# Forty-eight low-part subtractions on GpSimd, and GpSimd's loads on ScalarE's queue

## The reference

```python
def first_block(x, ...):
    for l in range(DEPTH):                       # DEPTH = 2
        h = rms_norm(x, norm_g[l])
        (gu, gv, gz, rq, rk, rv, rz, dq, dk, dv, dz,
         a_f, b_f, a_b, b_b) = jnp.split(h @ w_in[l], IN_OFFSETS, axis=-1)   # eleven blocks of 512 columns
        y_a = gmlp_branch(...)                   # token mixing with a 128x128 matrix
        y_b = retention_branch(...)              # rotary, decay masks, both directions
        y_c = gdn_branch(...)                    # delta rule: inverse of a 64x64 triangle, scan over 4 chunks
        proj = jnp.einsum("bsnw,nwd->bsnd", branches, w_branch_out[l])
        gates = jax.nn.sigmoid(jnp.einsum("bsd,dne->bsne", h, w_gate[l]))
        x = x + jnp.sum(gates * proj, axis=2) @ w_out[l]
    return rms_norm(x, final_norm_g)
```

## Time and profile before

| what | value |
|---|---|
| median of three runs | 1969.39 us |
| span of the profiled execution, its first to its last instruction (the page gives no other time of that execution) | 1968.4 us |
| TensorE (PE) busy | 1799.5 us, 91% |
| VectorE (DVE) busy | 1154.7 us, 59% |
| ScalarE (ACT) busy | 875.8 us, 44% |
| GpSimd (POOL) busy | 11.4 us, 1% |
| the 16 DMA engines | 148 GB/s on average |
| mean granted TensorE clock | 0.947 |

### The profile page before, as it was taken

The page is one execution under the profiler, slowest core; times in us unless marked ns, Lnnn a source line. Parts: engine busy times, 40 slices in busy tenths (PEclk is TensorE's granted clock), DMA queues, the critical chain, the costliest instruction groups (busy, mean ns, idle before and its releaser), DMA issues.

```text
span 1968.4 us, 24530 instructions
## 1 busy us (share of the span) xinstructions
PE 1799.5 (91%) x10424; PEld 1486.3 (76%) x10424; DVE 1154.7 (59%) x1578; ACT 875.8 (44%) x1017; POOL 11.4 (1%) x24
## 2 busy tenths in 40 slices
PE   7899899898999988999898989899989998769996
PEld 5777788687877876888686757788868886558885
DVE  4776885556778656545556534554555455774554
ACT  5443444346244434444445633444444444644442
POOL 0000000000000000000000000000000000000000
PEclk9899999888999998999899968899999998879998
DMA  6231445432123644555442212555545554234552
GB/s 253 84 108 66 145 154 192 160 129 86 67 102 129 226 152 150 187 187 192 161 171 99 94 43 94 184 186 192 192 164 191 190 193 160 94 131 171 174 189 86
DMA packets 41438, 291.75 MB, mean 148 GB/s; under 512 B 4609, under 2 KB 4737, under 8 KB 7153
## 3 DMA queue, kind: packets, MB, share of 16 engines
q1 hardware_dynamic: 38720, 280.16, 39.9%
q0 software_dynamic: 2608, 10.03, 1.4%
HBM read 289.12 MB, written 1.05 MB: 147 GB/s over the span
## 4 chain that ended last, share of the span: by engine, by line
PE 75%; DVE 16%; ACT 5%; issue 3%; POOL 0%; DVEq 0%; ACTq 0%
PE pg L436 22%; PE pg L437 21%; PE pg L438 21%; DVE wl L1383 4%; PE ps L634 3%; PE ps L516 2%; ACT wh L993 2%; DVE x L1841 1%; PE ps L889 1%; PE ps L887 1%; DVE arena L1504 1%; DVE arena L1507 1%; PE ps L674 0%; DVE arena L1999 0%; DVE sm L1460 0%
## 5 line engine op out<-in xcount | busy, mean ns | idle before, releaser
L1383 DVE TENSOR_TENSOR wl<-raw,wh 128x2048 fp32r<-128x2048 f32 x266 | 608.6, 2292 | 518.6 <-ACT wh L993 517.6
L436 PE MATMUL pg<-wh,hTh 128*128 128x512 f32 (+1 forms) x2160 | 852.4, 395 | 43.6 <-DVE hTl L1424 11.3
L437 PE MATMUL pg<-wl,hTh 128*128 128x512 f32 (+1 forms) x2160 | 836.9, 387 | 0.0
L438 PE MATMUL pg<-wh,hTl 128*128 128x512 f32 (+1 forms) x2160 | 835.9, 387 | 0.0
L993 ACT ACTIVATE wh<-raw 128x2048 fp32r<-128x2048 f32 x266 | 508.9, 1914 | 525.6 <-PE pg L438 516.7
L436 PEld LDWEIGHTS pg<-wh,hTh 128*128 128x128 f32 x2160 | 412.8, 191 | 138.6 <-issue 46.3
L438 PEld LDWEIGHTS pg<-wh,hTl 128*128 128x128 f32 x2160 | 411.6, 191 | 83.1
L437 PEld LDWEIGHTS pg<-wl,hTh 128*128 128x128 f32 x2160 | 412.3, 191 | 76.7
L1072 ACT ACTIVATE arena<-pg,sm 128x512 f32<-128x512 f32 (+1 forms) x49 | 33.0, 673 | 163.4 <-PE pg L438 163.4
L516 PE MATMUL ps<-cst,x 128*128 128x128 f32 x128 | 27.6, 402 | 50.7 <-DVE x L1841 34.1
L516 PEld LDWEIGHTS ps<-cst,x 128*128 128x128 f32 x128 | 24.6, 215 | 53.6 <-DVE x L1841 36.2
(11 more groups left out here) (320 smaller groups left out, 1168.9 us busy)
## 6 DMA issues: line engine op xcount, KB each, us to landing
raw<-weights SPq DMA_DIRECT2D x266, 1024.0 KB, 4.8
arena<-wide POOLq DMA_DIRECT2D x9, 512.0 KB, 3.5
x<-x_in SPq DMA_DIRECT2D x1, 1024.0 KB, 5.0
cst<-const_tables POOLq DMA_DIRECT2D x1, 1024.0 KB, 5.1
plainh<-dist_tables POOLq DMA_DIRECT2D x2, 512.0 KB, 4.8
arena<-gate_mix POOLq DMA_DIRECT2D x1, 1024.0 KB, 5.8
y_out<-x POOLq DMA_DIRECT2D x1, 1024.0 KB, 4.5
arena<-token_mix POOLq DMA_DIRECT2D x2, 256.0 KB, 3.8
```

Of the source, the lines that this page charges most:

```text
L436: pe.matmul(dst, lh, rh, start=first, stop=False)
L437: pe.matmul(dst, lh, rl, start=False, stop=False)
L438: return pe.matmul(dst, ll, rh, start=False, stop=last)
L1383: tt(wl[:, slot, :], raw[:, u % RAW_SLOTS, :], wh[:, slot, :], ALU.subtract)\
```

## The change

The 48 filler units' low parts are written by GpSimd instead of VectorE. The semaphore `split_low` becomes two, `low_dve` and `low_pool`, and TensorE and SyncE wait for the one that belongs to the unit. GpSimd's loads and its store move into ScalarE's program, at places where ScalarE's own order or an added wait makes them safe.

```diff
+LAYER_UNITS, FF_UNITS, HYB_UNITS, REC_UNITS = 44, 34, 30, 12
+POOL_UNITS = frozenset([LAYER_UNITS * l + u for l in range(DEPTH) for u in range(6, 22)]
+                       + [LAYER_UNITS * DEPTH + FF_UNITS + u for u in range(10, 22)]
+                       + [LAYER_UNITS * DEPTH + 3 * FF_UNITS + HYB_UNITS + u for u in range(4, 8)])
+def low_of(u):
+    by_pool = len([v for v in POOL_UNITS if v <= u])
+    return ("low_pool", by_pool) if u in POOL_UNITS else ("low_dve", u + 1 - by_pool)
...
 (TensorE, in prepare and gemm)
-                        pe.wait_ge(sem["split_low"], st.used + 1)
+                        low, count = low_of(st.used)
+                        pe.wait_ge(sem[low], count)
...
 (ScalarE)
+                if l == DEPTH - 1:
+                    act.dma_start(V(13824), wide[6]).then_inc(sem["final_g_landed"], 16)
                 gemm(D, (512,), ("evac_act",), read_gates(1, 1))
+                act.wait_ge(sem["params_used"], l + 1)
+                act.dma_start(par[:, :], params[l + 1]).then_inc(sem["params_landed"], 16)
...
+            def ffn(name, post, last_of_block=False):
                 features_of_x(lambda k: name[:, k:k + 1], X_AT)
+                load_gain(post)
+                if last_of_block:
+                    act.dma_start(V(11776, 2048).rearrange("p (t n) -> p t n", t=2),
+                                  gate_mix.rearrange("t p n -> p t n")).then_inc(sem["mix_landed"], 16)
+                    act.wait_ge(sem["params_used"], DEPTH + 1)
+                    act.dma_start(par[:, :], params[3]).then_inc(sem["params_landed"], 16)
...
 (hybrid and recurrent, behind features_of_x: load_gain(1), load_gain(4))
+            def load_gain(i):
+                act.dma_start(V(13824), wide[i]).then_inc(sem["wide_landed"], 16)
...
                 features_of_x(lambda k: fp("norm_g")[:, k:k + 1])
+                act.dma_start(DIST, dist).then_inc(sem["dist_landed"], 16)
                 small_w(16, fp("small_w"))
                 gdn()
+                act.dma_start(LN_GAINS, wide[7 + l]).then_inc(sem["wide_landed"], 16)
+                act.dma_start(TOKEN_MIX, token_mix[l]).then_inc(sem["mix_landed"], 16)
                 retention()
...
+            c.wait("x_ready", 2)
+            act.dma_start(out.rearrange("a (m p) d -> p (a m) d", p=P), x[:, :, :]).then_inc(sem["out_landed"], 16)
+            act.wait_ge(sem["out_landed"], 16)
...
 (VectorE, in pump)
-                    dve.wait_ge(sem["split_high"], u + 1)
-                    tt(wl[:, slot, :], raw[:, u % RAW_SLOTS, :], wh[:, slot, :], ALU.subtract)\
-                        .then_inc(sem["split_low"], 1)
+                    if u not in POOL_UNITS:
+                        dve.wait_ge(sem["split_high"], u + 1)
+                        tt(wl[:, slot, :], raw[:, u % RAW_SLOTS, :], wh[:, slot, :], ALU.subtract)\
+                            .then_inc(sem["low_dve"], 1)
...
 (SyncE)
-                    sp.wait_ge(sem["split_low"], u - RAW_SLOTS + 1)
+                    low, count = low_of(u - RAW_SLOTS)
+                    sp.wait_ge(sem[low], count)
...
 (GpSimd, behind its first two loads; its later loads and the store are gone from here)
+            for u in sorted(POOL_UNITS):
+                slot = u % SPLIT_SLOTS
+                pool.wait_ge(sem["split_high"], u + 1)
+                pool.tensor_tensor(wl[:, slot, :], raw[:, u % RAW_SLOTS, :], wh[:, slot, :], ALU.subtract)\
+                    .then_inc(sem["low_pool"], 1)
```

More of the change, by code:

```diff
@@ L276, in program @@
             "rope_done", "row_done", "rs_ready", "rv_ready", "sc_masked", "sc_ready", "small_done",
-            "small_read", "small_w_high", "small_w_low", "split_high", "split_low", "sq_done", "sq_free",
+            "small_read", "small_w_high", "small_w_low", "split_high", "low_dve", "low_pool", "sq_done", "sq_free",
             "sq_ready", "ssd_decay", "ssd_done", "ssd_mask", "state_ready", "state_scaled", "sv_done",
@@ L1183, in retention, with merge_out @@
                 prepare(4)
-            def merge_out():
+            def merge_out(l):
                 def read_gates(n, first=0):
@@ L1226, in gemm_out @@
                 pump(st.used + 3)
-            def ffn(name):
+            def ffn(name, post, last_of_block=False):
                 features_of_x(lambda k: name[:, k:k + 1], X_AT)
+                load_gain(post)
[4 more added lines that the diff above has]
+                    act.dma_start(par[:, :], params[3]).then_inc(sem["params_landed"], 16)
                 hid = V(0, 2 * FF).rearrange("p (m f) -> p m f", m=M)
@@ L1241, in hybrid @@
                 features_of_x(lambda k: spar("g2")[:, k:k + 1])
+                load_gain(1)
                 z = V(10240, 2048).rearrange("p (m f) -> p m f", m=M)
@@ L1315, in recurrent @@
                 features_of_x(lambda k: rp("g2")[:, k:k + 1])
+                load_gain(4)
                 def read(i, pair, w):
@@ L1355, in _ @@
                 features_of_x(lambda k: fp("norm_g")[:, k:k + 1])
+                act.dma_start(DIST, dist).then_inc(sem["dist_landed"], 16)
                 small_w(16, fp("small_w"))
                 gdn()
+                act.dma_start(LN_GAINS, wide[7 + l]).then_inc(sem["wide_landed"], 16)
+                act.dma_start(TOKEN_MIX, token_mix[l]).then_inc(sem["mix_landed"], 16)
                 retention()
-                merge_out()
+                merge_out(l)
             act.wait_ge(sem["params_landed"], 16 * 2)
             small_w(24, spar("small_w"))
-            ffn(spar("g0"))
+            ffn(spar("g0"), 0)
             hybrid()
-            ffn(spar("g4"))
+            ffn(spar("g4"), 2, True)
             act.wait_ge(sem["params_landed"], 16 * 3)
-            ffn(rp("g0"))
+            ffn(rp("g0"), 3)
             recurrent()
-            ffn(rp("g4"))
+            ffn(rp("g4"), 5)
+            c.wait("x_ready", 2)
+            act.dma_start(out.rearrange("a (m p) d -> p (a m) d", p=P), x[:, :, :]).then_inc(sem["out_landed"], 16)
+            act.wait_ge(sem["out_landed"], 16)
         @block.vector
@@ L2085, in _ @@
         def _(pool):
-            c = Counter(pool, sem, None)
             pool.dma_start(ident, const[:, 0:P]).then_inc(sem["ident_landed"], 16)
```

## The result

The change made the kernel slower: 2027.78 us median (2024.35 to 2033.16, four runs) against 1970.43 us (1969.28 to 1972.56) for the kernel before on the same chip. The ratio is 1.0292, interval 1.0274 to 1.0309. The forecast was 1986 us, with a range up to 2002. So the direction was right, and the size was too small by a factor of 3.5: 58.8 us more in the profiled span (2027.2 against 1968.4), where 16.9 were counted.

What follows compares the result with a forecast made beforehand. TensorE, busy 91% of the span, was taken to bound the kernel, low parts costing only where it waits. Span 1968.4 + 13.6 for two layers + 3.3 for the hybrid mixer + 1.0 around it gave 1986 us, range 1951 to 2002.

Steps and rivals of the forecast that it cites:

- GpSimd's 4.6 us: Filler units: time GpSimd takes for one low part, its two inputs coming in one after the other, 4.6 us.
- The loads at nothing: ScalarE's queue: eighteen moved transfers, about 6 us of issue, are hidden and cost nothing.
- Units with little room: Filler units with 4.55 to 4.8 us between high part and first use; the tightest gives back 0.6 us a layer.
- masks and start of the inverse: Each layer: GpSimd holds L1566's second operation, 2.2 us, and operations among L1577 to L1580, 2.3 us.
- waits that go: Each layer: TensorE's waits at L634, L674 and L690, met by no GpSimd operation, end; -2.1 us.
- scan's end: Each layer: L1634 with two SBUF inputs starts late behind GpSimd, TensorE waiting at its end; 2.0 us.
- rotary step: Each layer: two GpSimd units fall into two-input operations; one hold costs 0.1 us, two 4.7, middle 2.4.
- hybrid mixer: Four units beside sixteen heads: one mask hold of 2.2 us, the others 1.5 as mean, less 2.7 gained; +3.3 us.
- I take the middle: Start of the inverse: between nothing and a 4.6 us hold, 2.3 us; the rotary step likewise 2.4.
- far end: Each layer: the hold's upper values, 9.2 us in the inverse and 4.7 in the rotary step, making 16.0 us.
- recorded rival: Whole kernel: holds at 16.0 us a layer plus the hybrid's 3.3, 35 us, 2005 us; within the hold's 0.46 chance.
- The gain's cap: Whole kernel, VectorE undisturbed: 7.2 us a layer and 2.7 in the hybrid mixer, 17.1 us gained, 1952 us; chance 0.29.

Runs made afterwards that it cites:

- delay run: No low parts on GpSimd, three extra one-input VectorE reductions in each layer ahead of the small copy; ratio 1.0039 to the kernel before.
- loads-only trace: All low parts back on VectorE, GpSimd's eighteen transfers still on ScalarE's queue; 1969.4 us, ratio 0.9994 to the kernel before.
- copy from PSUM: The change, but with VectorE's small copy L1574 reading its source from PSUM instead of SBUF; 2016.78 us, ratio 1.0247 to the kernel before.
- free units' kernel: Only fifteen units, picked to meet no VectorE operation that can be held, on GpSimd; 1969.01 us, ratio 0.9988 to the kernel before.

## Why the prediction was wrong, step by step

**Right.** The mechanism: GpSimd's reads hold VectorE's two-input operations for the whole operation. The side taken in it: slower. GpSimd's 4.6 us: its median is 4.59, 4.5 to 4.6 where nothing is in its way, and up to 6.1 where VectorE got in first. The Trainium skill gives 4497 ns for it (GPSIMD Engine Reference, section 3.1, Elementwise), and the trace's median agrees within about 2%. The loads at nothing: 0.9994. Units with little room: TensorE waits for GpSimd's low part three times, 2.3 us in the whole run.

**Wrong: the size.** Here each term of the sum stands beside its shift in the first layer of the change:

| step | predicted | measured |
|---|---|---|
| small copies and scalar operations (no term) | 0 | +8.1 |
| masks and start of the inverse | 2.2 + 2.3 = +4.5 | +8.6 |
| waits that go | -2.1 | -2.7 |
| scan's end | +2.0 | +3.4 |
| rotary step | +2.4 | +4.9 |
| first layer | +6.8 | +22.3 |
| second layer | +6.8 | +17.1 |
| hybrid mixer | +3.3 | +16.9 |
| elsewhere | 0 | +2.5 |
| span | +16.9 | +58.8 |

- **A kind of operation was missing.** The prediction said that one-input lines would not show long instances. The copies L1574, L1586 and L1942 and the scalar operations of L1488 did. L1574 alone costs the first layer most of its 8.1 us, 3 of waiting and the rest slow matmuls; in the second layer it is held only 0.2 us. In the section that the prediction cites, "Who interferes with whom" of SBUF — State Buffer, the Trainium skill names this kind too: copies and scalar operations that run in a mode with two ports contend with GpSimd whatever it does. Half the rule was used. The runs bear out the other half: L1574 is held by a copy and by a memset, and not once it reads PSUM.
- **"I take the middle" for the inverse (2.3) and the rotary step (2.4).** The choice was one hold or none in the inverse, and two or one in the rotary step. In both places it was two: L1616 and L1614, L1706 and L1699. In the inverse the first hold made the second. In these traces GpSimd got its turn between two operations of such a row each time, so the far end was the likely value and not the bound: 9.2 in the inverse (8.6 were held) and 4.7 in the rotary step (8.6 were held, less the two low parts of 4.49 ahead) make 16.0 a layer, as in the recorded rival. Its 35 us in all were still short, as it had no copies in it and took the hybrid mixer at 3.3.
- **The masks (2.2).** This term was worked out well: the pair L1602 is held 4.4 us, less the low part of 2.3 that stood ahead of it.
- **The hybrid mixer (3.3).** Four heads were counted, at 2.2 and three times 1.3 or so. The mask is held in four heads, but 1.9 to 4.0 us each, 12.4 in all. Copy L1942 is held 4.3 and L1956 2.0. The "microsecond of room" of the other heads was read from one head. Alone this part costs 0.74%.
- **Slow matmuls were not in the sum.** TensorE's mean granted clock fell from 0.947 to 0.929; from 108 to 148 us of the changed kernel it was 0.75, where before had 0.94 over 100 to 130. How much of the 58.8 us is due to the clock is not settled: the delay run shows that part of it can be hidden. Of the +2.5 us "elsewhere", the slow matmuls ahead of unit 132 are 2.4, and the loads-only trace has them too.
- **The gain's cap was 21 to 23 us, not 17.1.** This error went the other way.
- **The base.** 1.0 us was kept for what lies around the span; the runs of the kernel before have 1.8 us between each time and its span.

As a whole the balance is: 21 to 23 us gained, 80.8 us held, and 57.4 us lost between the medians. That these fit so closely is partly chance, since "copy from PSUM" holds as much and ends 11 us earlier.

So the step that failed is the sum of the holds, +13.6 us for the two layers and +3.3 for the hybrid mixer: it took half holds where whole and double ones came, and counted nothing for held copies and the slow matmuls behind them. Measured were +39.4 and +16.9.

## What to carry to other kernels

Before moving work to GpSimd, list what VectorE runs in each window of GpSimd's operation: operations with two SBUF inputs, and SBUF-to-SBUF copies however small, wait for all of it. A long run of them is held more than once if the hold lets the next GpSimd operation start inside it. Move only units whose windows hold operations of the other kinds: the reduction L1561 keeps its 1.22 us beside a GpSimd subtraction, and L1688 with its PSUM input its 686 ns. Or give the disturbed operation a PSUM input, and look for the damage in the durations of VectorE's operations, not in its idle time.

## What the runs showed of the hardware that was not expected

- A copy of 128x16 between SBUF tiles took 3.91 us beside a GpSimd subtraction, 1.38 on average beside its memsets, and 0.17 when it read PSUM.
- Two-input operations keep 684 ns beside a GpSimd memset (1810 ns each), and take 2.38 us beside a one-input copy of GpSimd (1987 ns each).
- After a wait of 2.9 us TensorE took 3.68 us for 32 matmuls that otherwise take 1.96, whether GpSimd or a longer VectorE program made it wait. After the same wait in another kernel they took 2.15.
- Executions of one kernel fell into two groups 5 us apart, along with their granted clock: eight of the free units' kernel took about 1969 us with a mean of 0.940 to 0.942, three about 1964 us with 0.946 to 0.948. Its whole gain is 0.12%, 2.4 us.
